# A three-block fp32 layer stack on one core: block 1's recurrence preparation reordered, block 3's gate slabs moved

## The chip, the cores and the metric

The kernel runs on one NeuronCore of a Trainium2 chip. The metric is the device time of one execution in microseconds (us), lower is better. The engines are TensorE (PE in the profile; its weight loads are PEld), VectorE (DVE), ScalarE (ACT), GpSimd (POOL) and SyncE (SP). Each follows its own instruction stream in order and waits for the others on semaphores.

## The reference

The input is 512 tokens by 1024 features in float32. It goes through three layers ("blocks"), each a mixer and a feed-forward part. Cut to what the change touches:

```python
# block 1: sparse attention beside an RWKV7 recurrence
r, k, v, w_lo, a_lo, g_lo = split(z + mu * (z_prev - z))
w = -softplus(-(w0 + tanh(w_lo) @ w2)) - 0.5
a = sigmoid(a0 + a_lo @ a2);  g = sigmoid(g_lo) @ g2
kk = k * k_k;  kk = kk / max(sqrt(sum_head(kk * kk)), 1e-12)      # the key norm
k = k * (1 + (a - 1) * k_a);  decay = exp(-exp(w));  b = kk * a
state = state * decay + (state @ -kk) b + v k                     # per token
y = (norm(state @ r) * ln_w + ln_b + sum_head(r * k * r_k) * v) * g
merged = sigmoid(gate_attn) * (y_attn @ w_a) + sigmoid(gate_rwkv) * (y @ w_r)

# block 3: three mixers one after the other: mLSTM ("m"), GLA ("l"), gated DeltaNet ("d")
qkv = silu(causal_conv(dq, dk, dv));  gq, gk = l2norm(q) * P**-0.5, l2norm(k)
g_dec = -exp(a_log) * softplus(da + dt_bias);  beta = sigmoid(dbeta)
A = strict_lower(beta * (gk @ gk.T) * decay);  w, u = solve(I + A, [beta*gk*exp(b), beta*v])
x = x + (sum_n sigmoid(gate_n) * (branch_n @ up_n)) @ w_out
```

## The kernel before

Everything lies transposed: a tile `W(i)` holds 128 features by 512 tokens; `bank[0..7]` are the eight PSUM banks. A weight matrix comes in slabs of 128 x 1024 numbers. SP loads them in one fixed order (`stream`) into a ring of four. For each slab ScalarE makes a rounded high part (`high_part`, L1114), GpSimd subtracts it to get the low part (`low_parts`, L2716), and TensorE makes eight products out of it, each of three matmuls (high x high, high x low, low x high; L335, L336, L337). `dense` does one output tile per slab, in banks 0 to 3. Two slabs are always split ahead of the one in use (`LOOK = 2`); which slab ScalarE splits next is written into its own stream, so a slab is split late if ScalarE is held up.

Each block also needs gate tiles (16, 16 and 24). A gate tile is one slab, so eight products. They depend on nothing but the normalised input, and `early_gates(n)` puts n such products in between other work on TensorE. ScalarE's `send_gate` then splits the slab after the next, copies the finished gate to a staging tile and stores it by a DMA. How many products go where is a set of numbers: `IN_ATTENTION = 4` per attention step, `IN_MLSTM`, `IN_GLA`, `IN_GDN`, `IN_LEVEL`, `IN_STATE` in block 3, and `EARLY_M`, `EARLY_L` slabs counted in with the first two mixers; what is left comes before the merge.

Block 1: 32 attention steps carry all 16 gates. Then the recurrence is prepared: ScalarE applies tanh and sigmoid to the hidden layers (L1406 to L1408), TensorE multiplies them by the small matrices (L662 to L671), VectorE scans the decays (L2201) and forms their differences over all four tiles at once (L2205, L2208), then squares and sums of the keys are made (L2212, L1419, L442, L2217), the norm's Ln and Exp (L1423, L1426), the keys (L2224 to L2233), the decays' exponentials over four tiles (L1434 to L1438), and at last the operands, two of them on GpSimd (L2802, L2803) and the rest on VectorE (L2241, L2242). TensorE's first recurrence product is L696.

Block 3: after the slabs `in_m` come mLSTM's gate rows, transposes (L452) and four head steps (L865 to L890); after `in_l` GLA's 40 level steps (L934 to L946); after `in_d` (16 slabs) DeltaNet: convolutions (L2575, L2580), SiLU (L1766), squares (L1769), their sums (L442) and Ln (L1773), Exp (L1776), rows broadcast by TensorE (L972, L976) and copied by VectorE (L2614, L2617), operands (L2635 to L2637), the key products (L993), two inversions of six levels each (`merge_levels`: L533, a ScalarE copy L1461, `beside`, L556, VectorE's L2086), four state steps, a norm, the remaining gates and the merge. The decay row's softplus (L1749 to L1763) follows `in_d`'s copies on ScalarE.

## Time and profile before

| | |
|---|---|
| time before, median of 3 runs | 3276.92 us (3276.01 to 3278.44) |
| the profiled execution's own time | 3273.09 us |
| its span | 3271.3 us |
| TensorE busy | 2995.1 us (92%) |
| VectorE, ScalarE, GpSimd busy | 1405.6, 1155.8, 1205.4 us |

TensorE's busy time is near the span; its idle stretches and the stretches where its granted clock (PEclk, in tenths) is low lie in a few places. GpSimd's and ScalarE's idle time is mostly waiting for the next slab's turn.

### The profile page before, as it was taken

To read this page: it belongs to the slowest core of one execution; us is meant where nothing else is said; L and a number is where in the kernel's file an instruction comes from. 1 tells how busy PE (TensorE), PEld (TensorE's weight loads), DVE (VectorE), ACT (ScalarE), POOL (GpSimd) and SP (SyncE) were. 2 spreads that over 40 slices of the span, in tenths; PEclk is the share of its full clock that TensorE was granted. 3 is DMA by queue.
4 is the path that set the end of the run, shared out by engine and by line. 5 is a ranking of instruction groups with operands and counts; after the bars stand their busy time and mean duration, and the time that the engine had idled before them with its cause. 6 is when DMAs were issued, how large, how long until landed. Compare 5 with 4: busy or idle time off the path is not lost.

```text
span 3271.3 us, 40067 instructions
## 1 busy us (share of the span) xinstructions
PE 2995.1 (92%) x15600; PEld 2325.2 (71%) x15600; DVE 1405.6 (43%) x2024; ACT 1155.8 (35%) x1666; POOL 1205.4 (37%) x559
## 2 busy tenths in 40 slices
PE   7989967979999999889999999979889788999998
PEld 5856636858888886767888887746668466788886
DVE  3007736455221374432273445051376442665442
ACT  4244341344222336334342224233442623542222
POOL 3422512124444452424544443403214122544442
PEclk9998978989999999999999999978899799999999
DMA  3222210032333332225422222302112111622222
GB/s 123 96 77 65 68 30 2 3 130 96 97 97 97 105 128 81 90 74 169 146 95 93 97 97 91 109 23 72 54 49 97 45 40 58 216 97 96 92 96 84
DMA packets 80665, 284.05 MB, mean 87 GB/s; under 512 B 8968, under 2 KB 9096, under 8 KB 79744
## 3 DMA queue, kind: packets, MB, share of 16 engines
q1 hardware_dynamic: 66240, 236.36, 21.8%
q10 hardware_dynamic: 13296, 41.97, 3.4%
q0 software_dynamic: 976, 3.56, 0.4%
q8 instruction: 111, 1.82, 0.2%
q14 instruction: 42, 0.34, 0.0%
HBM read 260.86 MB, written 20.99 MB: 86 GB/s over the span
## 4 chain that ended last, share of the span: by engine, by line
PE 44%; issue 29%; POOL 13%; DVE 8%; ACT 4%; DMA 0%; POOLq 0%; SPq 0%; ACTq 0%; DVEq 0%
POOL slab_r L2716 13%; PE bank L335 11%; PE bank L337 11%; PE bank L336 11%; PE bank L556 2%; PE bank L442 1%; PE bank L533 1%; PE bank L610 1%; PE bank L944 1%; DVE work L2176 1%; DVE small L2174 1%; PE bank L883 1%; PE bank L452 0%; DVE work L2163 0%; PE bank L623 0%
## 5 line engine op out<-in xcount | busy, mean ns | idle before, releaser
L2716 POOL TENSOR_TENSOR slab_r<-slab,slab_high 128x1024 fp32r<-128x1024 f32 x442 | 1096.0, 2482 | 1697.3 <-ACT slab_high L1114 1697.1
L335 PE MATMUL bank<-xh,slab_high 128*128 128x512 f32 x2256 | 902.0, 400 | 30.1 <-POOL slab_r L2716 21.3
L337 PE MATMUL bank<-xh,slab_r 128*128 128x512 f32 x2256 | 884.7, 392 | 0.0
L336 PE MATMUL bank<-x_raw_r,slab_high 128*128 128x512 f32 x2064 | 811.0, 393 | 0.0
L1114 ACT CAST slab_high<-slab 128x1024 fp32r<-128x1024 f32 x442 | 462.3, 1047 | 453.3 <-DMA slab<-in_w_down 215.2
L336 PE MATMUL bank<-work_r,slab_high 128*128 128x512 f32 x1376 | 546.2, 397 | 0.0
L335 PEld LDWEIGHTS bank<-xh,slab_high 128*128 128x128 f32 x2256 | 428.2, 190 | 141.5 <-issue 26.0
L335 PE MATMUL bank<-work_r,slab_high 128*128 128x512 f32 x1184 | 474.7, 401 | 49.0 <-DVE work_r L1916 24.9
L337 PEld LDWEIGHTS bank<-xh,slab_r 128*128 128x128 f32 x2256 | 427.8, 190 | 92.7
L337 PE MATMUL bank<-work_r,slab_r 128*128 128x512 f32 x1184 | 474.7, 401 | 0.0
L336 PEld LDWEIGHTS bank<-x_raw_r,slab_high 128*128 128x128 f32 x2064 | 392.5, 190 | 79.8 <-issue 1.7
L336 PEld LDWEIGHTS bank<-work_r,slab_high 128*128 128x128 f32 x1376 | 260.9, 190 | 65.2 <-issue 1.4
L335 PEld LDWEIGHTS bank<-work_r,slab_high 128*128 128x128 f32 x1184 | 224.8, 190 | 111.1 <-issue 49.4
L337 PEld LDWEIGHTS bank<-work_r,slab_r 128*128 128x128 f32 x1184 | 224.9, 190 | 53.5
L1961 DVE TENSOR_TENSOR work_r<-work,work_r (+1 forms) x86 | 171.5, 1994 | 9.0
L1951 DVE TENSOR_TENSOR work<-work,bank 128x512 f32 x64 | 44.0, 687 | 285.7 <-PE bank L337 285.7
L442 PE MATMUL bank<-work,cst 128*128 128x512 f32 x110 | 69.0, 769 | 52.7 <-ACT work L1419 12.2
L1176 ACT COPY work<-bank 128x512 f32 x60 | 35.2, 587 | 227.4 <-PE bank L337 227.4
L1261 ACT ACTIVATE work<-bank 128x512 f32<-128x512 f32 x56 | 33.6, 600 | 222.8 <-PE bank L337 214.0
L1199 ACT ACTIVATE work<-work 128x512 f32<-128x512 f32 x56 | 35.4, 633 | 163.7 <-DVE work L1943 163.5
L1943 DVE TENSOR_TENSOR work<-work,bank 128x512 f32<-128x512 f32 x48 | 33.0, 687 | 135.7 <-PE bank L337 135.7
L2054 DVE TENSOR_TENSOR work<-work,bank 128x512 f32<-128x512 f32 x56 | 38.5, 687 | 115.7 <-ACT work L1542 76.6
(465 smaller groups left out, 2861.1 us busy)
## 6 DMA issues: line engine op xcount, KB each, us to landing
slab<-in_w_down SPq DMA_DIRECT2D x88, 512.0 KB, 3.2
slab<-in_w_up SPq DMA_DIRECT2D x64, 512.0 KB, 3.2
slab<-in_w_gates SPq DMA_DIRECT2D x56, 512.0 KB, 3.3
slab<-in_w_merge SPq DMA_DIRECT2D x48, 512.0 KB, 3.8
slab<-in_w_gu SPq DMA_DIRECT2D x44, 512.0 KB, 3.5
slab<-in_w_in_a SPq DMA_DIRECT2D x32, 512.0 KB, 3.5
gates<-staging ACTq DMA_DIRECT2D x56, 256.0 KB, 3.0
slab<-in_w_out SPq DMA_DIRECT2D x24, 512.0 KB, 3.2
```

Source lines behind the costliest of these rows:

```text
L335: first = pe.matmul(bank[b][:, :], wh, mh, start=start, stop=False)
L336: pe.matmul(bank[b][:, :], wh, ml, start=False, stop=False)
L337: end = pe.matmul(bank[b][:, :], wl, mh, start=False, stop=stop)
L442: ins = pe.matmul(bank[b][:, :], lhsT, t, start=(k == 0), stop=(k == len(tiles) - 1))
L556: ins = pe.matmul(bank[b][r, at(q)], W(lhs)[r, part(4 * hf + q)], W(rhs)[r, part(4 * hf + q)], start=True, stop=True)
L1114: act.copy(slab_high[:, slot, :], slab[:, slot, :]).then_inc(S("slab_high"), 1)
L1176: act.copy(dyn(dst, i * RING + b), bank[b][:, :]).then_inc(evac, 1)
L1199: act.activation(W(sq[1 + c % 2]) if c else W(sq[0]), W(x0 + c), ACT.Square)\
L1951: return dve.tensor_tensor(t, t, bank[b][:, :], ALU.add)
L1961: dve.tensor_tensor(low, raw, plain(high), ALU.subtract).then_inc(S("hidden_split"), 1)
L2054: dve.tensor_tensor(o, W(sg + nb * (j % 2) + g), bank[b][:, :], ALU.mult)\
L2716: pool.tensor_tensor(slab_low[:, slot, :], slab[:, slot, :], plain(slab_high[:, slot, :]), ALU.subtract).then_inc(S("slab_split"), 1)
```

## The change

**Block 1.** The attention carries the same 16 gates as before, and the preparation has no slab work beside it. ScalarE now squares the raw keys and makes the hidden layers inside the attention's second but last round, ahead of the last gate's send and of the last head's copy. The key norm's four sums come first on TensorE, all in bank 7, and their Ln and Exp before the small matrices' sigmoids. VectorE then goes tile by tile: scan, keys, r k, the two differences; ScalarE's exponentials follow tile by tile. The two products that GpSimd made are made by VectorE as its last step, and the recurrence starts after them. The small matrices are loaded at the attention's start, by three DMAs on GpSimd's queue behind the first bias, into tiles 12 to 14.

**Block 3.** `EARLY_M` goes from 3 to 5 and `EARLY_L` from 6 to 8: 16 products (two gates) stand right behind `in_m`'s slabs, 16 between GLA's second and third transpose. The third mixer takes 12 slabs, 16 gate products, the sums and the row broadcasts, then the last 4 slabs (`in_d_rest`, the output gate's tiles); one gate product follows each of the 16 key products; the values are transposed before them, the keys after. The levels carry no gate product (3 before each L556 until now), the state steps 8 instead of 4. That makes 24 products left for the end instead of 20. The decay row's softplus moves from behind `in_d` to ahead of `in_l`'s copies on ScalarE, and the GLA's last gate is sent before its last head's output.

On VectorE, in block 1 between the attention's last step and the first recurrence product, before (the scans, then the differences, then one tile's keys and the next's):

```order
L2201 SCALAR_TENSOR_TENSOR work<-cst,work 128x128 x16
L2205 TENSOR_TENSOR work<-work 128x2048
L2208 TENSOR_TENSOR work<-work 128x2048
L2212 TENSOR_SCALAR work<-work,vec 128x512 x4
L2217 TENSOR_SCALAR work<-bank 128x512 x4
L2219 TENSOR_SCALAR small<-vec 128x4
L2224 TENSOR_TENSOR work<-work 128x512
L2226 TENSOR_SCALAR work<-work,vec,small 128x512
L2229 TENSOR_TENSOR work<-work 128x512
L2231 TENSOR_TENSOR work<-work 128x512
```

and now (norm copies, then one whole tile):

```order
L2242 TENSOR_SCALAR work<-work,vec 128x512 x4
L2244 TENSOR_SCALAR small<-vec 128x4
L2250 TENSOR_SCALAR work<-bank 128x512 x4
L2256 SCALAR_TENSOR_TENSOR work<-cst,work 128x128 x4
L2259 TENSOR_TENSOR work<-work 128x512
L2260 TENSOR_SCALAR work<-work,vec,small 128x512
L2263 TENSOR_TENSOR work<-work 128x512
L2264 TENSOR_TENSOR work<-work 128x512
L2266 SCALAR_TENSOR_TENSOR work<-work,vec 128x512
L2269 TENSOR_TENSOR work<-work 128x512
L2272 TENSOR_TENSOR work<-work 128x512
```

The scan of four tiles (L2201) is cut into one tile's (L2256) with that tile's keys and differences behind it; the differences are 128x512 instead of 128x2048.

On TensorE in block 3, at the start of the first level, before:

```order
L993 MATMUL bank<-work 128x256 x16
L499 MATMUL bank<-cst,work 64x64 x16
L533 MATMUL bank<-work 64x64 x16
L335 MATMUL bank<-xh,slab_high 128x512
L336 MATMUL bank<-x_raw_r,slab_high 128x512
L337 MATMUL bank<-xh,slab_r 128x512
L335 MATMUL bank<-xh,slab_high 128x512
L336 MATMUL bank<-x_raw_r,slab_high 128x512
L337 MATMUL bank<-xh,slab_r 128x512
L335 MATMUL bank<-xh,slab_high 128x512
L336 MATMUL bank<-x_raw_r,slab_high 128x512
L337 MATMUL bank<-xh,slab_r 128x512
```

and now (L345 to L347 are one gate product):

```order
L1007 MATMUL bank<-work 128x256
L345 MATMUL bank<-xh,slab_high 128x512
L346 MATMUL bank<-x_raw_r,slab_high 128x512
L347 MATMUL bank<-xh,slab_r 128x512
L462 MATMUL bank<-cst,work 128x128 x16
L509 MATMUL bank<-cst,work 64x64 x16
L543 MATMUL bank<-work 64x64 x16
L566 MATMUL bank<-work 64x64 x32
L543 MATMUL bank<-work 64x64 x16
L566 MATMUL bank<-work 64x64 x32
```

The gate products stand between the key products (L993, now L1007) and no longer between a level's first and second half (L533 and L556, now L543 and L566); the 16 key transposes (L462) stand behind them.

On ScalarE in block 3, between the first mixer's last gate and the second mixer's slabs, before:

```order
L1114 CAST slab_high<-slab 128x1024
L1152 COPY staging<-bank 128x512
L1154 DMA gates<-staging 128x512
L1133 UNCONDITIONAL_BRANCH
L1133 ISA
L1114 CAST slab_high<-slab 128x1024
```

and now:

```order
L1133 CAST slab_high<-slab 128x1024
L1171 COPY staging<-bank 128x512
L1173 DMA gates<-staging 128x512
L1722 ACT_TABLE_LOAD
L1722 ACTIVATE work<-work 4x512
L1725 ACTIVATE work<-work,vec 4x512
L1728 ACTIVATE work<-work 4x512
L1730 ACT_TABLE_LOAD
L1730 ACTIVATE work<-work 4x512
L1732 ACTIVATE small<-vec 4x1
L1734 ACT_TABLE_LOAD
L1734 ACTIVATE work<-work,small 4x512
L1152 UNCONDITIONAL_BRANCH
L1152 ISA
```

The softplus of the decay row, with three table loads, stands ahead of the loop that splits and copies `in_l`.

The diff, cut to its core:

```diff
-EARLY_2, EARLY_M, EARLY_L = 7, 3, 6
...
+        AHEAD_M, AHEAD_L, IN_GDN, FIRST_D = 16, 16, (16, 16), 12
...
-                   ("w_gates3", EARLY_M, EARLY_L, DC), ("w_in_d", 0, 16, DC),
-                   ("w_gates3", EARLY_M + EARLY_L, 24 - EARLY_M - EARLY_L, DC), ("w_merge3", 0, 16, 0),
...
-        IN_ATTENTION, IN_SEQUENCE, IN_MLSTM, IN_GLA, IN_LEVEL, IN_STATE = 4, 0, 6, 1, 3, 4
+        IN_ATTENTION, IN_SEQUENCE, IN_MLSTM, IN_GLA, IN_LEVEL, IN_STATE = 4, 0, 6, 1, 0, 8
...
-        IN_GDN = (16, 32)
...
+            mark("key_sums")
+            for c in range(4):
+                sum_tiles([W(SQUARES + c)], 7, "dve", pair, S("kk_square"))
...
+                low_rank(c)
             for c in range(4):
-                sum_tiles([W(28 + c)], 4 + c % 2, "dve", pair, S("kk_square"))
-            for c in range(4):
-                sum_tiles([W(28 + c)], 4 + c, "dve", pair, S("rk_ready"))
+                sum_tiles([W(RK + c)], 4 + c, "dve", pair, S("rk_ready"))
...
+            early_gates(AHEAD_M)
...
             for t in range(NT):
+                if t == 2:
+                    early_gates(AHEAD_L)
...
-            dense("in_d", 16, DC, xnk, ["act"], None)
+            dense("in_d", FIRST_D, DC, xnk, ["act"], None)
...
             early_gates(IN_GDN[0])
...
+                for b, row in ((7, W(ROW)), (6, W(17))):
+                    if last[b]:
+                        pe.wait_ge(*last[b])
+                    pe.matmul(bank[b][:, :], sel[32:36, :], row[32:36, :], start=True, stop=True)\
+                        .then_inc(psum_for["dve"], hand(b, "dve"))
+            dense("in_d_rest", 16 - FIRST_D, DC, xnk, ["act"], None)
+            mark("gdn_slabs_done")
+            pe.wait_ge(S("kq_ready"), n.next(S("kq_ready")))
+            pe.wait_ge(S("values_scaled"), n.next(S("values_scaled")))
...
@@ -993,6 +1007,11 @@
                     pe.matmul(bank[b][:, 0:2 * P], W(22 + h)[:, ch * P:(ch + 1) * P], kq[:, h,
                         ch].rearrange("p s t -> p (s t)"), start=True, stop=True)\
                         .then_inc(psum_for["dve"], hand(b, "dve"))
+                    early_gates(1)
+            pe.wait_ge(S("operands_ready"), n.next(S("operands_ready")))
+            for t in range(NT):
+                cs = slice(t * P, (t + 1) * P)
+                tokens = turn([(W(34 + c)[:, cs], c * P) for c in range(4)], 4 + t % 2, "act")
...
+            def key_squares():
+                for c in range(4):
+                    act.wait_ge(S("kk_raw"), n.next(S("kk_raw")))
+                    act.activation(W(SQUARES + c), W(KEYS + c), ACT.Square)\
+                        .then_inc(S("kk_square"), n.up(S("kk_square")))
...
+            def hidden_layers():
+                act.wait_ge(S("shift_done"), n.next(S("shift_done"), 15))
+                act.activation(W(28)[0:HD, :], W(28)[0:HD, :], ACT.Tanh).then_inc(S("lora_ready"), n.up(S("lora_ready")))
+                act.activation(W(29), W(29), ACT.Sigmoid).then_inc(S("lora_ready"), n.up(S("lora_ready")))
+                act.activation(W(31)[0:32, :], W(31)[0:32, :], ACT.Sigmoid)\
+                    .then_inc(S("lora_ready"), n.up(S("lora_ready")))
...
+                if g == len(steps):
+                    key_squares()
+                    hidden_layers()
...
+            for c in range(4):
+                act.wait_ge(S("decay_sums"), n.next(S("decay_sums")))
+                act.activation(SM(4 * c, 4), w3(44 + c)[:, :, 63], ACT.Exp, scale=-EXPM05).then_inc(chain, n.up(chain))
+                act.wait_ge(chain, n.own(chain))
+                act.activation(W(40 + c), W(40 + c), ACT.Exp, scale=-EXPM05)\
+                    .then_inc(S("decays_ready"), n.up(S("decays_ready")))
+                act.activation(W(44 + c), W(48 + c), ACT.Exp, scale=-EXPM05)\
+                    .then_inc(S("decays_ready"), n.up(S("decays_ready")))
+                act.wait_ge(S("decays_ready"), n.own(S("decays_ready")))
+                act.activation(W(48 + c), W(48 + c), ACT.Exp, scale=EXPM05)\
+                    .then_inc(S("decays_ready"), n.up(S("decays_ready")))
...
+            send_gates(0, 32 + AHEAD_M // DC)
...
+            act.activation(W(ROW_WORK)[32:36, :], W(ROW_WORK)[32:36, :], ACT.Exp, scale=-1.0)\
+                .then_inc(chain, n.up(chain))
+            act.activation(SM(60)[32:36], V("alog")[32:36], ACT.Exp).then_inc(chain, n.up(chain))
+            act.wait_ge(chain, n.own(chain))
+            act.activation(W(ROW_WORK)[32:36, :], W(ROW_WORK)[32:36, :], ACT.Ln, bias=eps["one"][32:36])\
+                .then_inc(S("lf_parts"), n.up(S("lf_parts")))
...
+            early[1] += AHEAD_L
+            send_gates(0, 32 + EARLY_M + AHEAD_L // DC)
...
+            send_gates(0, 32 + EARLY_M + EARLY_L)
...
-            act.wait_ge(S("lf_parts"), n.own(S("lf_parts")))
-            act.wait_ge(S("conv3_done"), n.next(S("conv3_done")))
-            act.activation(W(18, 12), W(18, 12), ACT.Silu).then_inc(chain, n.up(chain))
+            copy_tiles("in_d", FIRST_D, W3(0, FIRST_D))
+            act.wait_ge(S("conv3_keys"), n.next(S("conv3_keys")))
+            act.activation(W(18, 8), W(18, 8), ACT.Silu).then_inc(chain, n.up(chain))
             act.wait_ge(chain, n.own(chain))
             for c in range(8):
                 act.activation(W(c), W(18 + c), ACT.Square).then_inc(S("qk_square"), n.up(S("qk_square")))
-            send_gates(0, 41 + IN_GDN[0] // DC)
+            act.wait_ge(S("conv3_done"), n.next(S("conv3_done")))
+            act.activation(W(26, 4), W(26, 4), ACT.Silu).then_inc(S("values_ready"), n.up(S("values_ready")))
+            send_gates(0, 32 + EARLY_M + EARLY_L + IN_GDN[0] // DC)
...
+            d0 = tiles("in_d_rest")
+            for t in range(16 - FIRST_D):
+                if t < 3:
+                    high_next()
+                act.wait_ge(psum_for["act"], d0 + t + 1)
+                act.copy(W(FIRST_D + t), bank[t % RING][:, :]).then_inc(evac, 1)
+                if t == 0:
+                    high_next()
+                    act.wait_ge(S("b_rows"), n.next(S("b_rows")))
+                    act.activation(W(38, 4), W(38, 4), ACT.Exp).then_inc(chain, n.up(chain))
+                    act.activation(W(42, 4), W(42, 4), ACT.Exp).then_inc(chain, n.up(chain))
+                    act.activation(W(46, 4), W(46, 4), ACT.Exp).then_inc(S("decays_ready"), n.up(S("decays_ready")))
...
+            for t in range(NT):
+                act.wait_ge(psum_for["act"], n.next(psum_for["act"]))
+                act.copy(W(VALUES[t]), bank[4 + t % 2][:, :]).then_inc(evac, n.up(evac))
+            early[1] = (32 + EARLY_M + EARLY_L) * DC + sum(IN_GDN)
+            send_gates(0, early[1] // DC)
...
             for c in range(4):
+                dve.tensor_scalar(W(KEYS + c), W(20 + c), V("kk", c), None, ALU.mult)\
+                    .then_inc(S("kk_raw"), n.up(S("kk_raw")))
...
+            for c in range(4):
+                dve.wait_ge(evac_by["act"], handed_at["rwkv"]["act"] + 3 * c + 2)
                 for t in range(NT):
...
                 dve.wait_ge(S("kk_rstd"), n.next(S("kk_rstd")))
...
+                dve.tensor_tensor(W(KEYS + c), W(KEYS + c), W(SQUARES + c), ALU.mult).then_inc(chain, n.up(chain))
...
+                dve.scalar_tensor_tensor(W(RK + c), W(16 + c), V("rk", c), W(20 + c), ALU.mult, ALU.mult)\
+                    .then_inc(S("rk_ready"), n.up(S("rk_ready")))
+                w3 = lambda i: W(i).rearrange("p (n t) -> p n t", n=NT)
+                dve.tensor_tensor(w3(48 + c), w3(44 + c), w3(44 + c)[:, :, 63:64].broadcast_to([P, NT, P]), ALU.subtract)\
+                    .then_inc(chain, n.up(chain))
...
+                dve.tensor_tensor(W(40 + c), W(48 + c), W(40 + c), ALU.subtract)\
+                    .then_inc(S("decay_sums"), n.up(S("decay_sums")))
...
+            dve.tensor_tensor(W(8, 4), W(52, 4), W(48, 4), ALU.mult).then_inc(chain, n.up(chain))
+            dve.tensor_tensor(W(12, 4), W(20, 4), W(48, 4), ALU.mult)\
+                .then_inc(S("operands_ready_2"), n.up(S("operands_ready_2")))
+            dve.wait_ge(S("operands_ready_2"), n.own(S("operands_ready_2")))
...
+            pool.wait_ge(evac_by["act"], handed_at["attention"]["act"])
+            for i, name, rows in zip(LOW_RANK, ("w2a2", "g2a", "g2b"), (P, P, 32)):
+                pool.dma_start(W(i)[0:rows, :], a[name]).then_inc(S("lora_loads"), 16)
...
-            pool.tensor_tensor(W(8, 4), W(52, 4), W(48, 4), ALU.mult).then_inc(chain, n.up(chain))
-            pool.tensor_tensor(W(12, 4), W(20, 4), W(48, 4), ALU.mult)\
-                .then_inc(S("operands_ready_2"), n.up(S("operands_ready_2")))
-            pool.wait_ge(S("operands_ready_2"), n.own(S("operands_ready_2")))
```

## Rows read from the trace of the kernel before

**Rows 1.** The page: busy, granted clock in 40 slices, the slab split's group.
```profile
PE 2995.1 (92%) x15600; PEld 2325.2 (71%) x15600; DVE 1405.6 (43%) x2024; ACT 1155.8 (35%) x1666; POOL 1205.4 (37%) x559
...
PEclk9998978989999999999999999978899799999999
...
L2716 POOL TENSOR_TENSOR slab_r<-slab,slab_high 128x1024 fp32r<-128x1024 f32 x442 | 1096.0, 2482 | 1697.3 <-ACT slab_high L1114 1697.1
```

**Rows 2.** Timeline, ScalarE, 424-522 us: start, length, engine, line, shape, count [idle before <-releaser].
```profile
433.02 0.26 ACT L1392 COPY work<-bank 64x128 f32<-64x128 f32 x1 [0.49 <-PE bank L639]
...
435.39 0.63 ACT L1406 ACTIVATE work<-work 64x512 f32<-64x512 f32 x1
...
437.86 0.61 ACT L1408 ACTIVATE work<-work 32x512 f32<-32x512 f32 x1
```

**Rows 3.** Timeline, TensorE, the same stretch.
```profile
496.32 2.04 PE L442 MATMUL bank<-work,cst 128*128 128x512 f32 x2 [1.38 <-DVE work L2233]
...
509.87 1.23 PE L696 MATMUL bank<-work 64*128 64x256 f32 x4 [11.51 <-DVE small L2243]
```

**Rows 4.** Timeline, VectorE, the same stretch.
```profile
461.58 5.58 DVE L2201 TENSOR_TENSOR_SCAN work<-cst,work 128x128 f32<-128x128 f32 x16 [33.53 <-ACT work L1416]
...
467.20 2.29 DVE L2205 TENSOR_TENSOR work<-work 128x2048 f32<-128x2048 f32 x1
...
482.39 0.69 DVE L2224 TENSOR_TENSOR work<-work 128x512 f32<-128x512 f32 x1 [2.78 <-ACT work L1426]
...
485.82 0.69 DVE L2224 TENSOR_TENSOR work<-work 128x512 f32<-128x512 f32 x1
...
496.84 4.98 DVE L2242 TENSOR_TENSOR work<-work 128x512 f32<-128x512 f32 x1
```

**Rows 5.** Timeline, GpSimd, the same stretch.
```profile
496.29 4.99 POOL L2802 TENSOR_TENSOR work<-work 128x2048 f32<-128x2048 f32 x1 [58.02 <-DVE small L2235]
```

**Rows 6.** Timeline, TensorE, the starts of block 3's first and second mixers.
```profile
2131.12 0.59 PE L452 MATMUL bank<-cst,work 4*128 4x4 f32 x4 [8.15 <-DVE work L2450]
...
2337.66 1.97 PE L452 MATMUL bank<-cst,work 128*128 128x128 f32 x8 [9.98 <-ACT work L1708]
```

**Rows 7.** Timeline, ScalarE, block 3's third mixer.
```profile
2453.36 1.05 ACT L1114 CAST slab_high<-slab 128x1024 fp32r<-128x1024 f32 x1 [5.97 <-DVE work L2570]
...
2461.46 0.59 ACT L1176 COPY work<-bank 128x512 f32 x1 [3.90 <-PE bank L337]
...
2537.62 0.59 ACT L1176 COPY work<-bank 128x512 f32 x1 [3.90 <-PE bank L337]
...
2548.38 5.32 ACT L1766 ACTIVATE work<-work 128x6144 f32<-128x6144 f32 x1
...
2553.73 4.27 ACT L1769 ACTIVATE work<-work 128x512 f32<-128x512 f32 x8
...
2561.72 1.28 ACT L1773 ACT_TABLE_LOAD   x1 [0.39 <-ACT staging L1152]
```

**Rows 8.** Timeline, TensorE, the third mixer up to its first level.
```profile
2447.53 0.77 PE L335 MATMUL bank<-xh,slab_high 128*128 128x512 f32 x1 [8.72 <-ACT staging L1152]
...
2563.76 8.38 PE L442 MATMUL bank<-work,cst 128*128 128x512 f32 x12 [5.51 <-ACT work L1773]
...
2648.37 1.92 PE L533 MATMUL bank<-work 64*64 64x64 f32 x32
```

**Rows 9.** Timeline, TensorE, one level of the inversion.
```profile
2661.84 0.50 PE L335 MATMUL bank<-xh,slab_high 128*128 128x512 f32 x1
...
2664.11 2.08 PE L556 MATMUL bank<-work 64*64 64x64 f32 x64
```

**Rows 10.** Timeline, VectorE, the third mixer's operands.
```profile
2608.15 2.83 DVE L2637 TENSOR_TENSOR work<-work 128x512 f32<-128x512 f32 x1
...
2616.50 0.68 DVE L2637 TENSOR_TENSOR work<-work 128x512 f32<-128x512 f32 x1
...
2617.11 0.68 DVE L2635 TENSOR_TENSOR work<-work 128x512 f32<-128x512 f32 x1
```

263 lines of the change are left out of this document (105 added, 158 removed).

## The prediction

> **What bounds the kernel now.** I read the page first. TensorE is busy 2995.1 us of a 3271.3 us span, so 276 us are its idle time, and the granted clock is 0.7 or 0.8 of full in eight of the forty slices [rows 1]. The other engines are under half busy. Time is therefore won only where TensorE stands still or where its products run at the lower clock. Then I read the timelines of block 1's preparation and of block 3's third mixer, engine beside engine, because there lie the edits. In block 1, TensorE's last waits before the recurrence end with VectorE: 11.51 us for the operands [rows 3]. In block 3 there are waits of 8.15 and 9.98 us at the starts of the first two mixers [rows 6], and 8.72 and 5.51 us in the third [rows 8]. A slab product has a fixed price, since ScalarE copies tile after tile in step with TensorE: from tile 1 (2461.46) to tile 15 (2537.62) are 76.16 us for 14 slabs, 5.44 us a slab, 0.68 us a product [rows 7]. The change neither adds nor removes a product, it moves them. Moved into a wait a product costs nothing; taken from a place with no wait it gives 0.68 us back; put in such a place it costs that.
>
> **Block 1, the preparation.** The attention has the same gates, so its steps stay. Ahead of the recurrence everything hangs on one chain, which I rebuild with the rows' durations. The copy at 433.02 ends at 433.3. ScalarE now squares the keys (eight squares take 4.27 us [rows 7], so four 2.1), makes the hidden layers (435.39 to 437.86 + 0.61, 3.1 us), then sends the gate and makes the last head's copy (what stands between 433.3 and 435.39, 2.1 us) [rows 2]: 440.6. The last head's copy frees bank 7, in which all key sums lie. A sum takes 2.04 us at the clock granted there [rows 3], a copy out of the bank 0.69 (as every 128x512 operation of VectorE [rows 4]), and with one bank they alternate: 4 x 2.73 = 10.9, to 451.5. Ln, a table load (1.28 [rows 7]), four Exps, another table load, two sigmoids (each 0.6): 0.6 + 1.3 + 2.4 + 1.3 + 1.2 = 6.8, to 458.3 or, with the semaphores between, 458.9. VectorE then takes per tile a quarter of the scan (5.58 / 4 = 1.4), the keys (485.82 - 482.39 = 3.43) and two differences of 0.69 [rows 4], together 6.1 less 0.1, as such operations follow each other at a pitch below their length: 458.9 + 24.4 = 483.3. ScalarE's exponentials follow a tile behind, and the last ones (2.2 us) lie beside the operands of the first three tiles. The last r k sum ends at 484.1, eight operands at a pitch of 0.61 (2617.11 - 2616.50 = 0.61 [rows 10]) take 4.9, and the two large products, 2.29 each on VectorE by the 128x2048 row of the same form [rows 4], 4.6: 493.7 against 509.87 [rows 3]. That is **-16 us**, between -12 and -19: the ladder at full clock would be 2 us shorter, and 4 us are for the semaphores between four engines. Of it, 8.6 is certain by itself: beside GpSimd's product of 4.99 us [rows 5] VectorE's 128x512 multiplication lasted 4.98 us [rows 4] instead of 0.68 [rows 10], twice, and GpSimd makes none now. The loads of the small matrices stand on GpSimd's queue ahead of the second bias: **+0.5** (0 to 1.6).
>
> **The rule on the port.** The Trainium skill, SBUF — State Buffer, section "Terms", calls the port pair of VectorE and GpSimd an exclusive lock, where the loser is blocked for the whole instruction. The rows agree: 4.98 beside 4.99, and 2.83 beside a slab split whose mean is 2.48 [rows 1, 10]. It speaks against the new third mixer, where VectorE's operands stand beside the splits of eight slabs: each may cost 2.15 us more.
>
> **Block 3, first two starts.** 16 products take 10.9 us. At the first start they fill a wait of 8.15 [rows 6] and push it by 2.7; two gates must be sent on ScalarE, each 1.9 us (two lie between 2553.73 + 4.27 = 2558.00 and 2561.72 [rows 7]), of which I take 1.2 as exposed: **+3.9** (2 to 5). At the second start the wait is 9.98 [rows 6]; the products follow idle time, and at the lower clock they take up to 18, and 3.7 us of sends stand on ScalarE ahead of the level work: **+7** (3 to 12). The decay row's softplus, some 7.6 us on ScalarE with two table loads more than needed, now stands ahead of `in_l`'s copies. TensorE goes on until its four banks are full and the two slabs that were split ahead are used; that hides some 3 us: **+4.5** (3 to 7.6).
>
> **Third mixer, up to the first level.** The GLA's last gate is sent earlier, so the 8.72 us wait [rows 8] goes; but the third slab's split still waits for the last output's use (2453.36, behind a wait for VectorE [rows 7]), and that is next: **-6.8** (-4 to -8). The twelfth tile's copy then ends at 2461.46 + 10 x 5.44 + 0.6 - 6.8 = 2509.7. Call this T. Before, T to the first level took 2648.37 [rows 8] - 2516.5 = 131.9 us, with four slabs and 48 products in it (54.4 us). Now I follow ScalarE: SiLU over 4096 columns instead of 6144 (5.32 x 2/3 = 3.5), squares 4.27, SiLU of the values 1.9, the sends 3.7, two table loads: 16.6; then the Lns alternate with the sums: T + 26.5. The row broadcasts are bound by VectorE, 4 heads x 4 operations of 0.69: T + 36.5 with the wait behind them. Four slabs, 21.8: T + 58. VectorE has 32 operations at 0.61 and three or four collisions of 2.15 (2.83 - 0.68 [rows 10]), so masks start at T + 65.5; 16 key products with a gate product each at 0.95 us: T + 80; the key copies, the pack and the last mask 7.3: T + 87.5. So 88 instead of 132: **-44** (-30 to -50). As a cross-check, TensorE's own work in it is 21.8 of slabs, 21.8 of products, sums (12 matmuls of 8.38 [rows 8] for six of the eight: 11), broadcasts 10, the rest 13, together 78 of 88. So there are 10 us that no better overlap could take without a faster TensorE, and 88 isn't far from the floor.
>
> **The levels.** Each of the 12 gives up three products: from 2661.84 to 2664.11 are 2.27 us [rows 9], in all **-27**. What is late next? The first half's copy on ScalarE (some 0.6 to 1 us) must stand between L533 and L556; its columns are copied in parts while L533 runs, and VectorE's update of the former level is behind L556. If a wait of 1.7 us takes the products' place, only 7 us are left. I take the full 27, since in block 1's recurrence levels of this shape run back to back (the page's eighth slice, 572 to 654 us, lies in them and has a granted clock of 0.9 [rows 1]).
>
> **State steps and the end.** 4 x 4 more products, 16 x 0.68 = **+10.9**: VectorE's and ScalarE's copies there were already covered by four. Twenty-four instead of 20 products for the end, **+2.7**, and the fourth gate's send and split there **+2.8**.
>
> Sum: -16 + 0.5 + 3.9 + 4.5 + 7 - 6.8 - 44 - 27 + 10.9 + 5.5 = -61.5. The profiled execution took 3273.1 us, the median is 3276.9, so 3211.6 and **3215 us**.
>
> **The rivals.** (A) The sum as it stands: 0.66.
> (B) *A wait takes the place of the levels' products.* -27 becomes -7: 3235. For it: L556 needs what ScalarE copies from L533, and nothing else stands between them now. Against it: the copy is small, and L533 comes in 32 parts [rows 8]. 0.14.
> (C) *The third mixer is bound by VectorE and GpSimd.* With the low parts of eight slabs beside VectorE's operands each collision costs 2.15; at eight instead of three or four, and the two starts at their upper ends (+6), +10 + 6 and 4 us of softplus: 3235. For it: three of the old operands in a row were hit. 0.13.
> (D) *The idle time only moves.* Block 1's -16 stays, the rest gives nothing: 3260. Against it: the old 132 us hold 54 of slabs and products and TensorE's rows show waits of 5 to 6 us in them; it would need every filled wait to open again. 0.04.
> (E) *Slower: TensorE falls to the lower clock where the products are taken out.* The granted clock falls to 0.7 and 0.8 in slices with idle time [rows 1]. If all 12 levels ran at 1.2 GHz instead of 2.4 (3.3 us more each, L533 and L556 together [rows 8, 9]: 40), the state steps with 32 products and the matmuls between too (34), and the end's 24 products (16), it is 90 - 61: 3306. It decides from where 61 us of work at the full clock fall to half. Against it: 32 to 64 small matmuls in each half of a level leave no gap. 0.03.
> The Trainium skill, TensorE: Matmul & The Clock Gate, section "HAM oscillation — how this bites in real kernels", says that waits between groups of matmuls bring the clock down again; by that rule (B) would turn into (E), and the trace agrees as far as the slices with waits go.
>
> **How the numbers follow.** The forecast's own range is 3203 to 3230, from the bounds of the third mixer and the starts. With (B) and (C) the range is 3198 to 3240, and what is left out is (D), (E) and the far ends. A measurement tells 0.2% (6.5 us) from no change. (A), (B), (C) and nearly all of (D) are faster: 0.95; within 0.2% 0.02, the weak side of (D); slower 0.03, (E).
>
> **What would show it.** The first L696 (now L706) at 494, not 510; key sums from 441 on, in steps of 2.7. L2242's 4.98 us gone. In block 3 no TensorE wait over 3 us at the mixers' starts; the third mixer's twelfth tile to its first level 88 us; a level of some 3.5 us with no wait between its halves, and PEclk at 9 there. Wrong I would be if ScalarE's row in front of `in_l` leaves TensorE idle for its full 7.6 us, if a wait for a copy stands in each level, or if VectorE's operands in the third mixer show more than four lengths near 2.8.

## The result

| | median | runs |
|---|---|---|
| before | 3276.47 us | 4 (3274.95 to 3278.44) |
| changed | 3218.56 us | 4 (3211.78 to 3225.98) |
| ratio | 0.983, 95% interval 0.9806 to 0.9855 | |

The forecast was 3215 (3198 to 3240). The profiled execution of the changed kernel took 3222.05 us, 51.0 less than the profiled one of before; the medians lie 57.9 apart. The runs of one kernel now spread by 14 us, and where that comes from is a result of its own, below.

The page of the changed kernel, as [rows 1] of before: busy time, TensorE's busy tenths and its granted clock in 40 slices.

```profile
span 3220.2 us, 40009 instructions
...
PE 2983.3 (93%) x15600; PEld 2327.9 (72%) x15600; DVE 1420.0 (44%) x2031; ACT 1157.7 (36%) x1680; POOL 1194.8 (37%) x557
...
PE   6989987979999999898999999987988987999998
...
PEclk9987988989999999999999999988999889999999
```

TensorE works 11.8 us less with as many instructions. Its idle time goes from 276 to 237 us: that is where most of the gain is.

### The ledger of the two traces

TensorE's matmuls are the same in both kernels apart from their place, so I lined up the matmuls of the two profiled executions and read at each landmark (such as the first recurrence product) how much earlier or later the changed kernel gets there. What changes from one landmark to the next is the measured value of one term of the prediction's sum; a minus is time gained.

| stretch | forecast | measured |
|---|---|---|
| up to the attention's end | +0.5 | +3.8 (-0.8 up to the attention's first matmul, +4.6 in it) |
| block 1's preparation, to the first recurrence product | -16 | -17.0 |
| recurrence to the end of block 2 | 0 | +2.5 |
| first mixer, products ahead and head steps | +3.9 | +6.6 |
| second mixer's slabs | +4.5 | +5.7 |
| second mixer's start and levels | +7 | +2.1 |
| third mixer, 12 slabs | -6.8 | -4.2 |
| from there to the first level | -44 | -37.9 |
| 12 levels | -27 | -30.4 |
| state steps | +10.9 | +12.3 |
| the end's products | +5.5 | +6.0 |
| sum | -61.5 | -50.5 |

### Block 1's preparation

The timeline of the changed kernel, ScalarE, TensorE and VectorE, one fence each; they answer to [rows 2 to 4].

```profile
436.86 0.26 ACT L1411 COPY work<-bank 64x128 f32<-64x128 f32 x1 [0.49 <-PE bank L649]
...
462.26 0.68 ACT L1444 ACTIVATE work<-bank,vec 128x512 f32<-128x512 f32 x1
```

```profile
444.31 2.08 PE L452 MATMUL bank<-work,cst 128*128 128x512 f32 x2 [5.99 <-ACT work L1411]
...
447.24 2.08 PE L452 MATMUL bank<-work,cst 128*128 128x512 f32 x2 [0.86 <-DVE work L2250]
...
496.69 1.23 PE L711 MATMUL bank<-work 64*128 64x256 f32 x4 [9.71 <-issue]
```

```profile
462.97 1.37 DVE L2256 TENSOR_TENSOR_SCAN work<-cst,work 128x128 f32<-128x128 f32 x4 [7.20 <-ACT work L1444]
...
468.74 1.36 DVE L2256 TENSOR_TENSOR_SCAN work<-cst,work 128x128 f32<-128x128 f32 x4
...
491.29 0.69 DVE L2282 TENSOR_TENSOR work<-work 128x512 f32<-128x512 f32 x1
492.10 2.29 DVE L2287 TENSOR_TENSOR work<-work 128x2048 f32<-128x2048 f32 x1
```

From the last but one head's copy (its end at 437.12) to the first recurrence product (496.69) are 59.6 us; before they were 433.28 to 509.87, 76.6 [rows 2, 3]. The steps are those of the prediction, moved by the 3.8 us by which the attention ended later. A step of the sums is 2.86 us (the starts are 447.24, 450.10 and 452.96; the first step is 2.93), not 2.73, and a tile of VectorE's 5.77 (462.97 to 468.74), not 6.1. No operand takes 4.98 us any more. From the first operand to the first recurrence product were 13.6 us (496.23 to 509.87) and are 9.6 (487.07 to 496.69): the two held operations are 8.6 us less, and the two large products, which VectorE now makes itself, are 4.6 more. So the ports are worth 4.0 of the 17, and the other 13 come with the new order of the steps; no run changes that order alone.

### Block 3

TensorE at the start of the second mixer's slabs, at the 12 slabs of the third, and between there and the first levels.

```profile
2232.83 0.77 PE L345 MATMUL bank<-xh,slab_high 128*128 128x512 f32 x1 [4.47 <-ACT staging L1171]
...
2458.49 0.79 PE L345 MATMUL bank<-xh,slab_high 128*128 128x512 f32 x1 [5.05 <-POOL slab_r L2761]
...
2582.41 1.93 PE L462 MATMUL bank<-cst,work 128*128 128x128 f32 x8 [3.71 <-ACT work L1832]
...
2586.11 0.59 PE L1007 MATMUL bank<-work 128*128 128x256 f32 x2
2587.24 0.59 PE L1007 MATMUL bank<-work 128*128 128x256 f32 x2
...
2609.94 1.97 PE L543 MATMUL bank<-work 64*64 64x64 f32 x32 [2.38 <-POOL work L2780]
...
2617.39 1.48 PE L543 MATMUL bank<-work 64*64 64x64 f32 x32
2618.68 2.06 PE L566 MATMUL bank<-work 64*64 64x64 f32 x64
2620.57 1.46 PE L543 MATMUL bank<-work 64*64 64x64 f32 x32
```

A level takes 3.18 us (2617.39 to 2620.57) with no wait between its halves, where one with its three products took 5.6 (the products 2.27 of it [rows 9]). So rival (B) isn't what happened. The third mixer's start has lost the wait of 8.72 [rows 8], and the third slab's split is late next, as forecast. The first level starts 93.9 us after the end of the twelfth tile's copy (2516.04), not 88.

The windows from there to the first level, before and now (span of the window, busy times of TensorE, its weight loads, VectorE, ScalarE and GpSimd, granted clock, DMA share, GB/s):

```profile
2516.00:2648.00 132.00, 100.46 (x365) 65.34 (x365) 62.27 (x109) 64.26 (x78) 27.15 (x12) 0.83 0.15 52
```

```profile
2516.00:2610.00 94.00, 81.24 (x323) 56.43 (x323) 56.85 (x103) 50.94 (x65) 21.64 (x10) 0.87 0.16 57
```

TensorE stood still for 31.5 of 132 us and does so for 12.8 of 94. Of the 38 us some 19 are therefore filled idle time, 10.9 are the 16 products (at 0.68 each) that now stand elsewhere and are paid for there, and the other 8 are less busy time for the same work, at a granted clock of 0.87 instead of 0.83.

### The profile page after: what moved, and what is told of

Read it like the earlier page. It is cut to its first block, busy times and chain, and to the rows that moved or that the text cites. A ratio compares the mean times of both kernels' runs of the same rounds, so it can differ in the third digit from the quotient of the medians.

```text
span 3220.2 us, 40009 instructions
## 1 busy us (share of the span) xinstructions
PE 2983.3 (93%) x15600; PEld 2327.9 (72%) x15600; DVE 1420.0 (44%) x2031; ACT 1157.7 (36%) x1680; POOL 1194.8 (37%) x557
## 3 DMA queue, kind: packets, MB, share of 16 engines
q1 hardware_dynamic: 66240, 236.36, 22.1%
## 4 chain that ended last, share of the span: by engine, by line
PE 38%; issue 36%; POOL 15%; DVE 7%; ACT 3%; DMA 1%; POOLq 0%; SPq 0%; ACTq 0%; DVEq 0%
POOL slab_r L2761 15%; PE bank L345 10%; PE bank L347 9%; PE bank L346 9%; PE bank L566 2%; DVE work L2220 1%; PE bank L452 1%; PE bank L543 1%; DVE small L2218 1%; DVE work L2207 1%; PE bank L620 1%; PE bank L899 1%; PE bank L462 0%; DVE work L2530 0%; PE bank L633 0%
## 5 line engine op out<-in xcount | busy, mean ns | idle before, releaser
L345 PE MATMUL bank<-xh,slab_high 128*128 128x512 f32 x2256 | 906.0, 402 | 30.4 <-POOL slab_r L2761 21.4
L347 PE MATMUL bank<-xh,slab_r 128*128 128x512 f32 x2256 | 886.5, 393 | 0.0
L345 PEld LDWEIGHTS bank<-xh,slab_high 128*128 128x128 f32 x2256 | 429.8, 190 | 140.7 <-issue 26.4
L345 PE MATMUL bank<-work_r,slab_high 128*128 128x512 f32 x1184 | 472.7, 399 | 51.6 <-DVE work_r L1960 25.0
L347 PEld LDWEIGHTS bank<-xh,slab_r 128*128 128x128 f32 x2256 | 428.9, 190 | 93.2
L347 PE MATMUL bank<-work_r,slab_r 128*128 128x512 f32 x1184 | 473.4, 400 | 0.0
L345 PEld LDWEIGHTS bank<-work_r,slab_high 128*128 128x128 f32 x1184 | 224.2, 189 | 112.7 <-issue 48.6
L347 PEld LDWEIGHTS bank<-work_r,slab_r 128*128 128x128 f32 x1184 | 224.2, 189 | 52.7
```

The source lines that it names most:

```text
L345: first = pe.matmul(bank[b][:, :], wh, mh, start=start, stop=False)
L347: end = pe.matmul(bank[b][:, :], wl, mh, start=False, stop=stop)
```

## The experiments

Each is read twice: by its median beside the changed kernel's (3218.6 and, run again, 3216.1), and by the ledger of its trace against another of the same kernels, which is sharper. From the end of block 2 on, stretches of unchanged code agree within 0.2 us in most traces; the exceptions are told in the last section. The medians come from four series, each with its own runs of the kernel before (3276.47, 3273.36, 3275.03 and 3271.92 us), so a few us between medians of different series mean nothing.

### Each block alone, the loads moved, and the changed kernel again

`b1only` has the changed block 1 and the old block 3, `b3only` the other way round. `loads_late`:

```diff
-            pool.wait_ge(evac_by["act"], handed_at["attention"]["act"])
-            for i, name, rows in zip(LOW_RANK, ("w2a2", "g2a", "g2b"), (P, P, 32)):
-                pool.dma_start(W(i)[0:rows, :], a[name]).then_inc(S("lora_loads"), 16)
             for g in range(len(steps)):
...
+            for i, name, rows in zip(LOW_RANK, ("w2a2", "g2a", "g2b"), (P, P, 32)):
+                pool.dma_start(W(i)[0:rows, :], a[name]).then_inc(S("lora_loads"), 16)
             low_parts(AFTER_ATTENTION - early[0])
```

> Block 1 of the changed kernel with block 3 of the old one. Theory: the two parts add up; the preparation's chain gives 17 us (the changed kernel's trace has 59.6 us from the copy of the last but one head to the first recurrence product, where the old one has 76.6), the attention costs between 0 and 6, so 3276.5 - 11 to -17: 3260 to 3266. Rival: the attention ran longer only by chance of the clock in the one profile; then 3259 to 3261, at the fast end, and its profile shows the attention's end at 433 us and not at 437. Second rival: block 1's gain is given back later by the matmuls' clock in the recurrence: 3270.

> Block 3 of the changed kernel behind block 1 of the old one. Theory: from the ledger of the two traces block 3 gives 3 x -10.8 apart, -50.6 + 10.8 = -39.8: 3236.5. Rival, by the prediction's sum: -61.5 + 15.5 = -46: 3230. If the spread of the changed kernel's runs (3212 to 3226) comes from block 3, this kernel has it too; if from block 1, its runs lie within 4 us, as those of the old kernel do.

> The changed kernel with the three loads of the small matrices behind the attention's last step on GpSimd's queue, and not behind the first bias. Theory: the loads cost under 1 us at the attention's start, and what was longer there (6 us in the profile, with no wait but products at the lower clock) is the clock's: the time stays within 3 us of the changed kernel's median, 3218.6. Rival: the issues on GpSimd's queue delay the second bias and with it the first softmax, and TensorE falls to the lower clock for it: then 5 us less, 3213, and runs within 4 us of each other.

> The changed kernel once more, for a second profile and more times. If the 6 us in the attention are chance, this profile's attention ends at 433 us or at another time than 437, and the time follows it one for one; if they belong to the kernel, it ends at 437 again.

Measured: `b1only` 3259.24 us (3253.1 to 3259.7, 5 runs), `b3only` 3228.49 (3224.4 to 3232.0, 4 runs), `loads_late` 3216.30 (3214.5 to 3218.4, 4 runs), the changed kernel again 3216.09 (3211.8 to 3221.7, 4 runs), all beside 3273.36 of before (3265.3 to 3276.9, 8 runs). The old kernel spreads by 12 us here too.

Block 1 alone gives 14.1 and block 3 alone 44.9, together 59.0, and both together gave 57.3: **the two parts add up**. The ledgers say it more sharply: the preparation is 17.0 us shorter in `b1only`, and in `b3only` every stretch of block 3 is as long as in the changed kernel within 0.2 us, but for +0.4 in the levels and +0.6 at the end. `b1only`'s 14.1 lie in the theory's 11 to 17; its attention ends late too (436.6), so its rival's sign, 433, isn't there. For `b3only` the theory said -39.8 and the rival -46, and the median's -44.9 seems to favour the rival. Its ledger doesn't: block 3 gives 39.4 there, and the other 5.4 are what its attention happened to gain in that execution (8.8) less what its recurrence happened to lose (3.4). The rival's number came by luck.

The loads' place costs nothing that shows. The longer attention (4.6 us in the ledger, "6" in the expectations) is chance. The same attention code ran at different clocks in the profiles; the windows of three traces (columns as above): the changed kernel, the changed kernel again, and `b3only`.

```profile
245.00:312.00 67.00, 61.97 (x192) 37.85 (x190) 45.40 (x124) 24.51 (x63) 17.52 (x19) 0.75 0.21 62
```

```profile
245.00:312.00 67.00, 65.71 (x219) 40.56 (x219) 47.46 (x141) 27.19 (x68) 19.75 (x21) 0.80 0.23 65
```

```profile
245.00:312.00 67.00, 61.27 (x236) 39.05 (x235) 55.06 (x152) 27.76 (x72) 19.74 (x19) 0.97 0.21 67
```

At 0.97 TensorE gets 236 matmuls done in the window, at 0.75 192. The last but one head's copy ended 7.9 us earlier in the second profile than in the first of the very same kernel (429.20 and 437.12), and 12.7 earlier in `b3only`'s. My expectation for the second profile ("433 or another time") left both open; what it rules out is that the 437 belongs to the kernel. The stretch from the recurrence to the end of block 2 was 2.5 us shorter in the second profile too, as long as before, so the ledger's +2.5 there is chance as well. With both, the second profile's execution took 3211.76 us, 10.3 less than the first. Hence the difference between the profiled pair (51.0) and the medians (57.9), and hence the spread; neither edit alone takes it away (6.6 us in `b1only`, 7.6 in `b3only`).

### Products back in the levels

```diff
-        IN_ATTENTION, IN_SEQUENCE, IN_MLSTM, IN_GLA, IN_LEVEL, IN_STATE = 4, 0, 6, 1, 0, 8
+        IN_ATTENTION, IN_SEQUENCE, IN_MLSTM, IN_GLA, IN_LEVEL, IN_STATE = 4, 0, 6, 1, 3, 4
```

> The changed kernel with three gate products again in each of the 12 levels, four in each state step, and so four at the end. The number of products is the same. Theory: a product costs 0.68 in the state steps and at the end, and 0.84 in a level, where its place also broke the run of small matmuls (the two traces: -30.3 for 36 products). So +30.3 for the levels, -16 x 0.68 = -10.9 for the state steps, -20 x 0.68 = -13.6 for the end: +6. Rival (B of the prediction): the levels now wait for ScalarE's copies, and the products would fill those waits: -7 or better. Rival: products are worth the same everywhere: 0.

Measured: 3223.50 us (3219.4 to 3227.8, 4 runs), +4.9 on the first and +7.4 on the second series of the changed kernel. The ledger: levels +30.7, state steps -12.3, the end -12.0, net +6.4. That is the theory's +6, and rival (B) is off the table: no product in a level fills anything. But it also says how little of the -30 is won: a product costs 0.85 in the levels (36 of them), 0.77 in the state steps (16) and 0.60 at the end (20). Taking the 36 out was worth 6 us; the rest of the prediction's -27 is paid back elsewhere.

### No products ahead of the mixers

```diff
-EARLY_2, EARLY_M, EARLY_L = 7, 5, 8
+EARLY_2, EARLY_M, EARLY_L = 7, 3, 6
...
-        AHEAD_M, AHEAD_L, IN_GDN, FIRST_D = 16, 16, (16, 16), 12
+        AHEAD_M, AHEAD_L, IN_GDN, FIRST_D = 0, 0, (16, 16), 12
```

> The changed kernel without the 16 products ahead of the first and the 16 ahead of the second mixer; the 32 stand at the end instead. Theory: by the trace the first 16 cost 5.9 where they stand, the second 16 cost 2.1 (they fill waits of 8.15 and 9.98), and 32 at the end cost 32 x 0.68 = 21.8: +14. In the trace the first mixer's head steps start 5.9 earlier, the levels of the second 2 more. Rival: the sends and the slab splits that the products bring cost more than they save: 0 to +5.

Measured: 3232.18 us (3226.9 to 3233.2, 4 runs), some +15. The ledger against the changed kernel's trace: -7.0 up to the third mixer (-4.8 at the first two stretches, -2.2 at the second mixer's start), +22.1 at the end. So 32 products cost 7 us where they stand and 22 at the end. The theory's +14 held. One thing in it I had not expected: the second mixer's slabs were as late as with the products, though the wait of 4.47 us was not there; see the two locks below.

### One product back on GpSimd

```diff
-            dve.tensor_tensor(W(12, 4), W(20, 4), W(48, 4), ALU.mult)\
...
+            pool.wait_ge(S("decays_ready"), n.next(S("decays_ready"), 12))
+            pool.tensor_tensor(W(12, 4), W(20, 4), W(48, 4), ALU.mult)\
```

> The changed kernel with one of the two 128x2048 products of block 1 on GpSimd, beside VectorE's operands; the other stays on VectorE. Theory: the two engines hold one another, GpSimd's 4.99 us stand against all but one or two of VectorE's operations, so one 128x512 operation takes about 5 us: +4.3 for it, -2.3 for the product that VectorE no longer makes: from the last tile's keys to the first recurrence product +2. Rival: they overlap: -2.3.

Measured: 3225.96 us (2 runs), 7 to 10 above the changed kernel. More of that is the attention and the recurrence, slow in its profile (granted clock 0.75 from 245 to 312 us), than the edit; the edit is read from the stretch alone. VectorE and GpSimd in its trace:

```profile
491.45 0.69 DVE L2282 TENSOR_TENSOR work<-work 128x512 f32<-128x512 f32 x1 [0.65 <-ACT work L1468]
492.06 4.98 DVE L2283 TENSOR_TENSOR work<-work 128x512 f32<-128x512 f32 x1
```

```profile
491.56 4.93 POOL L2846 TENSOR_TENSOR work<-work 128x2048 f32<-128x2048 f32 x1 [45.49 <-ACT work L1468]
```

The stretch is 2.2 us longer (ledger), as the theory had it: the product costs 4.93 on GpSimd and one of VectorE's 128x512 operations stands still for it, 4.98 instead of 0.69. By the Trainium skill, SBUF — State Buffer, section "Terms", the pair of ports is an exclusive lock held for the whole instruction. The trace agrees.

### The second mixer's slabs: two locks on one door

The changed kernel loses 5.7 us there. I took that for the softplus. `softplus_shared` makes it beside the first mixer's own:

```diff
...
             act.activation(W(20)[0:4, :], W(19)[0:4, :], ACT.Abs).then_inc(chain, n.up(chain))
+            act.activation(W(ROW_WORK)[32:36, :], W(ROW)[32:36, :], ACT.Abs).then_inc(chain, n.up(chain))
             act.wait_ge(chain, n.own(chain))
             act.activation(W(20)[0:4, :], W(20)[0:4, :], ACT.Exp, scale=-1.0).then_inc(chain, n.up(chain))
+            act.activation(W(ROW_WORK)[32:36, :], W(ROW_WORK)[32:36, :], ACT.Exp, scale=-1.0)\
+                .then_inc(chain, n.up(chain))
...
```

> The changed kernel with the decay row's softplus and sigmoid made beside the first mixer's own, with its table loads, and not ahead of the second mixer's slabs. Theory: the 5.9 us at the second mixer's slabs go, and at the first mixer's start come 1 to 2 for the six small operations (ScalarE had 2.4 us of slack there, TensorE's 16 products cover the rest): -4 to -5. Rival: what cost 5.9 there was the gate's send and the lower clock after the head's end, not the softplus: -1 to +2.

Measured: 3219.20 us (3217.0 to 3221.1, 4 runs), no gain, as the rival had it; from the last head's products to the end of the slabs +1.2, over all of block 3 up to there -0.3 to -0.4. The wait for the gate's copy is still there with 4.47 us. The last gate ahead of these slabs is the 37th (counted over the three blocks), so it lies in bank 0 (`t % 4`), and the first slab's product needs bank 0. ScalarE copies it out behind the last head's Ln and Exp with their two table loads. `early_send` sends it ahead of them and leaves the softplus where it is:

```diff
                 act.activation(W(44), W(43), ACT.Square).then_inc(S("h_square"), n.up(S("h_square")))
+                if h == 3:
+                    send_gates(IN_MLSTM)
+                    send_gates(0, 32 + EARLY_M)
                 act.wait_ge(psum_for["act"], n.next(psum_for["act"]))
...
```

> The changed kernel with the first mixer's last gate sent ahead of its last head's Ln and Exp; the softplus stays ahead of the second mixer's slabs. That gate is the 37th, so it lies in bank 0, and the second mixer's first tile needs bank 0: TensorE's 4.47 us wait ends with that gate's copy. Theory: the wait shrinks to 1 or less (-3.5), but then the third slab's split comes late, because the softplus (7.6 us) stands ahead of it on ScalarE: some 2 of it come back, and the segment from the last head to the tenth tile gains 1 to 2. Rival: the lower clock behind the wait was the greater part; it goes too, and the segment gains 5 to 6.

Measured: 3217.00 us (2 runs), at the slabs -0.2: neither the theory's 1 to 2 nor the rival's 5 to 6. TensorE and ScalarE in its trace:

```profile
2223.57 0.47 PE L345 MATMUL bank<-xh,slab_high 128*128 128x512 f32 x1 [0.39 <-ACT staging L1171]
...
2238.87 0.50 PE L345 MATMUL bank<-xh,slab_high 128*128 128x512 f32 x1 [4.13 <-POOL slab_r L2764]
```

```profile
2235.35 1.05 ACT L1133 CAST slab_high<-slab 128x1024 fp32r<-128x1024 f32 x1 [0.17 <-ACT work L1737]
```

The 4.47 is gone, and a wait of 4.13 for the third slab has come, whose split ScalarE makes only when the softplus is done. Each of the two delays hides the other. With both edits in one kernel (`best`, below) the same stretch is 6.3 us shorter, and TensorE has no wait over 0.4 us in it. In `no_ahead` the last gate ahead is the 35th and lies in bank 2, and TensorE waits 3.75 us at these slabs for the third slab (and 0.88 for the second, as before the change): there it was the softplus alone.

### Slabs split further ahead, and ScalarE's order

`look` splits the third slab of the third mixer ahead of the last head's output and the fourth ahead of the wait for the norm; one gate's send then splits none.

```diff
             send_gates(0, 32 + EARLY_M + EARLY_L)
+            high_next()
             head_out(3)
...
+            high_next()
             act.wait_ge(S("h_used"), n.next(S("h_used")))
...
```

> The changed kernel with two more slabs split ahead of the third mixer (the third ahead of the last head's output, the fourth ahead of the wait for the norm's use). TensorE has one 5.05 us wait there now, for the third slab, and the products behind it run at the lower clock. Theory: the start is bound by the split alone, so 12 slabs take near 65.3 us instead of 73: -5 to -8 in that segment. Rival: the copies out of the banks wait for the same norm, so the fifth tile waits instead: -1 to -2.

Measured: 3215.21 us (2 runs). The 12 slabs are 7.5 us shorter, the theory's 5 to 8, and then 3.8 are given back. The line of ScalarE at the end of the 12 slabs says why:

```profile
2506.10 1.05 ACT L1133 CAST slab_high<-slab 128x1024 fp32r<-128x1024 f32 x1 [3.83 <-DMA slab<-in_w_in_d]
```

With three slabs ahead, ScalarE waits 3.83 us for a load before it may copy the twelfth tile, and SiLU and everything behind it come late.

`ladder_later` mends ScalarE's order in four places and puts the key sums into two banks:

```diff
                 if g == len(steps):
                     key_squares()
+                elif g > len(steps):
                     hidden_layers()
-                send_gates(IN_ATTENTION if g < len(steps) else 0)
+                if g != len(steps):
+                    send_gates(IN_ATTENTION if g < len(steps) else 0)
...
-                sum_tiles([W(SQUARES + c)], 7, "dve", pair, S("kk_square"))
+                sum_tiles([W(SQUARES + c)], 4 if c % 2 else 7, "dve", pair, S("kk_square"))
...
-            act.activation(W(12, 4), W(12, 4), ACT.Silu).then_inc(chain, n.up(chain))
-            act.wait_ge(chain, n.own(chain))
             for t in range(NT):
                 act.wait_ge(psum_for["act"], n.next(psum_for["act"]))
                 act.copy(W(VALUES[t]), bank[4 + t % 2][:, :]).then_inc(evac, n.up(evac))
+            act.activation(W(12, 4), W(12, 4), ACT.Silu).then_inc(chain, n.up(chain))
```

> The changed kernel with ScalarE's order mended in four places. Block 1: the last head's copy ahead of the hidden layers and of the gate's send, and the key sums in two banks in turn. Theory: the first sum starts 4 us earlier, the sums follow at 2.05 instead of 2.86 us (-2.4): -6 up to the first recurrence product; rival: the sigmoids wait for the hidden layers, which now stand behind: -3. First mixer: two gates sent behind the first head's exponentials: -3 of the 5.9; rival 0, if the head waits for VectorE. Third mixer: the output gate's SiLU behind the values' copies: -3.7 at the first key product; rival 0.

Measured: 3205.47 us (3202.9 to 3211.2, 4 runs), against the changed kernel's 3216 to 3219. TensorE in block 1:

```profile
438.08 5.42 PE L452 MATMUL bank<-work,cst 128*128 128x512 f32 x8 [1.22 <-ACT work L1411]
...
486.66 1.23 PE L711 MATMUL bank<-work 64*128 64x256 f32 x4 [9.71 <-issue]
```

The preparation is 8.6 us shorter (theory 6): the four sums take 5.42 in one run instead of four steps of 2.86, less than the theory's 4 x 2.05 as some of them ran at the higher clock. At the first mixer the later sends gave nothing (+0.2), as the rival had it; TensorE's waits in the heads end with VectorE. Moving the SiLU gave 4.5 up to the first level (theory 3.7), of which the levels give 0.5 back.

> All of these together, with the softplus beside the first mixer's own. Theory: block 1 -6, first mixer -3 + 1.4, second mixer's slabs -6 (with the softplus gone the third slab's split is in time), third mixer's start -6, its SiLU -3.7: -23 against the changed kernel, 3194. Rival: each gain ends at the next wait: -10, 3207.

`best` has the edits of `softplus_shared`, `early_send`, `look` and `ladder_later` in one kernel. Measured: **3196.39 us** (3186.3 to 3202.8, 5 runs), ratio to before 0.9769 (0.9749 to 0.9790). It beats both kernels: 20 us under the changed one, whose ratios to before were 0.983, and 75 under the old one. The ledger: block 1's preparation -7.8, the second mixer's slabs -6.3, its start -0.8, the third mixer's slabs -7.5, and from there to the first level -2.5 (the SiLU's 4.5 less what the late twelfth copy costs). Together -24.9 against a theory of -23. The first mixer's term, -3 + 1.4 in the theory, gave -0.1. That a gain ends at the next wait, as the rival had it, holds for `look` and there in part: 1.8 us of the SiLU's gain go to the late twelfth copy.

## Why the prediction was right, and where it wasn't

**The number and its luck.** 3215 was forecast and 3218.6 measured, and the second profile of the changed kernel is even 61.4 us shorter than the one of before. That is closer than the mechanism deserves. Leaving out the attention and the recurrence, where the same code differs from run to run, the other terms sum to -62.0 as forecast and -56.8 as measured. The single misses add up to 14.5 us one way and 9.3 the other, and cancel in part. The range, 3198 to 3240, was wide enough for all of them together.

**Block 1**, -16 against -17.0: the chain held step by step. What I called certain by itself, the 8.6 us of the ports, is what VectorE's operands lose; with the 4.6 for the two products, which stand in the same sum, it is 4.0. `pool_product` agrees: one held operation and one product less on VectorE make +2.2.

**Attention**, +0.5 against +3.8 up to its end: nothing of it shows as the loads' (`loads_late`). The step that failed is that I gave no range to the clock in code that the change doesn't touch. The same code takes up to 12 us more in one execution than in another there, and a single profiled execution doesn't tell. With the recurrence's +2.5, which is chance too, it is 5.8 of the 11.0 us between -61.5 and -50.5; against the medians the miss is 3.6.

**First mixer**, +3.9 against +6.6: the step that failed is where it is paid. The products ahead push the first head by only 1.4 us (2.7 forecast), and the head steps take 5.1 more. `no_ahead` takes back 4.7 of the 6.6. What remains, some 2 us in the head steps, is TensorE waiting for VectorE: 12.4 us in the last three heads against 8.9 before, and 12.7 in `no_ahead`. So it isn't the products'; what it is stays open, and moving the sends didn't touch it.

**Second mixer's slabs**, +4.5 against +5.7: the size was right and the reason only half. I read the softplus and overlooked that the two gates more move the last one into bank 0. Where the softplus stands alone, in `no_ahead`, TensorE waits 3.75 of its 7.6 us, so the slack is 3.8 and not 3, and the stretch still loses 5.7: the other 2 us are mostly the 0.63 us matmuls behind the wait (0.39 in full run), which I had not priced.

**Second mixer's start**, +7 against +2.1: the 16 products ran at the full clock but for the first five matmuls (all 48 in 12.2 us) and not the "up to 18" that I had allowed, and the wait of 9.98 [rows 6] hid nearly all. The slab splits did hit VectorE, as forecast for the third mixer: 5.42 us for two operations beside GpSimd's 5.14 for two splits.

```profile
2343.05 5.42 DVE L2573 TENSOR_TENSOR work<-work 128x512 f32<-128x512 f32 x2
```

```profile
2342.78 5.14 POOL L2761 TENSOR_TENSOR slab_r<-slab,slab_high 128x1024 fp32r<-128x1024 f32 x2 [21.63 <-ACT slab_high L1133]
```

**Third mixer's slabs**, -6.8 against -4.2: right that the third slab's split is next. That slab starts 6.4 us earlier, and then takes 7.7 us instead of 5.44, because the products behind its wait of 5.05 ran at the lower clock; these 2.3 I had not priced. My sign "no TensorE wait over 3 us at the mixers' starts" didn't come: there are 4.47 and 5.05, and 4.49 behind the second mixer's transposes.

**Third mixer, to the first level**, -44 against -37.9: two terms were mis-sized, as far as the trace tells. The output gate's SiLU stands ahead of the values' copies on ScalarE, a table load and 1.91 us that my walk along ScalarE left out (TensorE waits 3.71 for it; `ladder_later` gets 4.5 back), and a key product with its gate product takes 1.13 us (2586.11 to 2587.24), not 0.95: 16 times 0.18 are 2.9. Together they are 6.6, where 6.1 are missing. Of this stretch only the SiLU's place was changed by itself (`ladder_later`); its other parts, which make up the largest term of the sum, were tried only all together, in `b3only`. Rival (C) didn't come: VectorE's operands show three lengths of 2.8 to 2.9, the three or four that the sum had and not eight.

**Levels, state steps and end**: -27, +10.9 and +5.5 against -30.4, +12.3 and +6.0. The prices per product were 0.1 too low in the levels and the state steps alike, so the two misses cancel in part.

**Rivals.** (B) is excluded by the trace and by `levels_filled`. (D) is excluded by TensorE's idle time, 39 us less. (E) did not come in the changed kernel: the granted clock is 0.89 and 0.92 in its two runs of levels (0.96 and 0.94 before) and 0.97 in the state steps. In `softplus_shared` it came once, in small: the granted clock of the state steps was 0.90, and they took 3.0 us more than in the others at 0.97, with no edit near. The Trainium skill, TensorE: Matmul & The Clock Gate, section "HAM oscillation — how this bites in real kernels", has waits between matmul groups bring the clock down. The traces agree behind the waits of 4.47 and 5.05 us, where the first matmul took 0.77 to 0.79 us against 0.50 in full run and some ten followed at the lower clock. Behind the 4.13 of `early_send` the first two still ran at full clock, and eight at the lower clock came then.

## What to carry to other kernels

Count work that is moved by what it costs in its new place minus what it cost in its old one, and check the sum by TensorE's idle time: here 36 products came out of the levels for 30 us and most of that was paid again elsewhere. When a delay has two causes in a row, taking away either shows nothing; the sign is in the trace, where the old wait stays in full (`softplus_shared`) or one with another name takes its place (`early_send`). And follow the engine that copies and splits through its whole order, each activation with its table loads: what stood in the way at the end were single operations of ScalarE that nobody waited for, ahead of copies that TensorE waited for.
